# A two-block transformer on one core: from looped stages and three weight slots to an unrolled job list, five to eight slots and products that stream 512 weight columns

## The reference

```python
for l in range(2):                                    # first block
    x = layer_norm(ALPHA * x + 0.5 * swiglu(x, ffn1_w_gu[l], ffn1_w_down[l]))   # d_ff = 2816
    x = layer_norm(ALPHA * x + hybrid_mixer(x, w_in[l], w_out[l]))   # window attention + retention, w_in 1024x2816
    x = layer_norm(ALPHA * x + 0.5 * swiglu(x, ffn2_w_gu[l], ffn2_w_down[l]))
for l in range(2):                                    # second block, conditioned by c
    shift, scale, gate = split(silu(c) @ w_ada[l] + b_ada[l])
    h = x * (1 + scale) + shift
    p = h @ w_in_2[l]          # 4584 columns: latents, keys, queries, values, indexer, gate
    # latent attention (6 heads), dilated attention (6), top-64 sparse attention (4)
    y = concat(o_a, o_b, o_c) * silu(p_gate)
    x = layer_norm(ALPHA * x + (1 + gate) * (y @ w_out_2[l]))
```

## Time and profile before

| what | value |
|---|---|
| runs | 1542.51, 1539.28, 1542.38 us; median 1542.38 us |
| profiled execution | span 1539.8 us from the first to the last instruction; mean granted TensorE clock 0.988 |
| what lies around the span | 2.6 us, median of the runs less the span |
| PE busy | 1476.3 us, 96% of the span |
| PE weight loads | 1393.8 us, beside the products |
| DVE busy | 959.0 us, 62% |
| ACT busy | 621.4 us, 40% |
| POOL busy | 146.5 us, 10% |
| DMA | 265.49 MB, mean 172 GB/s |

### The profile page before, as it was taken

How to read it: one execution, slowest core, us unless ns; L and a number is a source line. 1 busy time by engine, 2 the same in 40 slices (tenths; PEclk the granted TensorE clock), 3 DMA queues, 4 the chain that set the end, 5 groups by cost and what they waited for, 6 DMA issues and landing times.

```text
span 1539.8 us, 29184 instructions
## 1 busy us (share of the span) xinstructions
PE 1476.3 (96%) x10900; PEld 1393.8 (91%) x10900; DVE 959.0 (62%) x1198; ACT 621.4 (40%) x754; POOL 146.5 (10%) x175
## 2 busy tenths in 40 slices
PE   8999999999999989999999999999999898999896
PEld 8999989889999989999898899999899896999794
DVE  2667665476677546676654766775657655567555
ACT  2434435523433414343355234333245463245551
POOL 1011010410011010100104100110100000000000
PEclk9999999999999999999999999999999999999998
DMA  7767645336767536676453366676453263453430
GB/s 247 230 215 232 216 150 168 111 110 212 228 209 231 184 131 227 218 232 215 148 171 110 110 212 226 212 230 200 158 172 113 78 206 97 136 184 96 126 120 28
DMA packets 195769, 265.49 MB, mean 172 GB/s; under 512 B 14992, under 2 KB 171152, under 8 KB 195168
## 3 DMA queue, kind: packets, MB, share of 16 engines
q1 hardware_dynamic: 183664, 222.51, 44.5%
q0 software_dynamic: 11728, 39.62, 8.4%
q10 hardware_dynamic: 288, 2.10, 0.4%
HBM read 263.13 MB, written 1.07 MB: 172 GB/s over the span
## 4 chain that ended last, share of the span: by engine, by line
PE 47%; issue 45%; POOL 5%; DVE 2%; DMA 1%; POOLq 0%; ACT 0%; DVEq 0%
PE ps L578 15%; PE ps L576 15%; PE ps L577 15%; PE ps L584 2%; POOL small L1653 1%; PE ps L716 1%; DVE x L1305 1%; POOL arena L1697 1%; PE ps L660 1%; POOL small L1726 1%; DMA mod_rows<-mod 0%; POOL arena L1698 0%; POOL arena L1699 0%; DVE arena L1555 0%; POOL arena L1695 0%
## 5 line engine op out<-in xcount | busy, mean ns | idle before, releaser
L1246 DVE TENSOR_TENSOR w_lo<-w_raw,w_hi 128x2048 fp32r<-128x2048 f32 (+3 forms) x224 | 489.2, 2188 | 261.5 <-ACT w_hi L995 257.2
L576 PE MATMUL ps<-col_hi,w_hi 128*128 128x256 f32 (+1 forms) x1744 | 493.6, 283 | 2.3 <-DVE w_lo L1246 2.3
L577 PE MATMUL ps<-col_lo,w_hi 128*128 128x256 f32 (+1 forms) x1744 | 492.3, 282 | 0.0
L578 PE MATMUL ps<-col_hi,w_lo 128*128 128x256 f32 (+1 forms) x1744 | 492.3, 282 | 0.0
L995 ACT ACTIVATE w_hi<-w_raw 128x2048 fp32r<-128x2048 f32 (+3 forms) x224 | 404.9, 1809 | 144.5 <-PE ps L578 140.6
L576 PEld LDWEIGHTS ps<-col_hi,w_hi 128*128 128x128 f32 x1744 | 334.9, 192 | 5.6 <-issue 3.3
L577 PEld LDWEIGHTS ps<-col_lo,w_hi 128*128 128x128 f32 x1744 | 335.0, 192 | 1.4
L578 PEld LDWEIGHTS ps<-col_hi,w_lo 128*128 128x128 f32 x1744 | 335.0, 192 | 0.0
L576 PE MATMUL ps<-w_hi,col_hi 128*128 128x256 f32 (+2 forms) x832 | 254.6, 306 | 4.1 <-DVE col_lo L1257 3.8
L577 PE MATMUL ps<-w_lo,col_hi 128*128 128x256 f32 (+2 forms) x832 | 250.2, 301 | 0.0
L578 PE MATMUL ps<-w_hi,col_lo 128*128 128x256 f32 (+2 forms) x832 | 250.1, 301 | 0.0
(11 more groups left out here) (150 smaller groups left out, 1240.3 us busy)
## 6 DMA issues: line engine op xcount, KB each, us to landing
w_raw<-in_ffn_w_gu SPq DMA_DIRECT2D x88, 1024.0 KB, 5.6
w_raw<-in_w_in SPq DMA_DIRECT2D x54, 1024.0 KB, 5.4
w_raw<-in_ffn_w_down SPq DMA_DIRECT2D x44, 1024.0 KB, 4.9
mod<-in_w_ada POOLq DMA_DIRECT2D x32, 768.0 KB, 5.3
w_raw<-in_w_out SPq DMA_DIRECT2D x16, 1024.0 KB, 4.9
norm_g<-in_ln_g POOLq DMA_DIRECT2D x8, 512.0 KB, 4.1
norm_b<-in_ln_b POOLq DMA_DIRECT2D x8, 512.0 KB, 5.6
w_raw<-in_w_uq SPq DMA_DIRECT2D x6, 576.0 KB, 4.0
```

The costliest lines, as they stand in the source:

```text
L576: pe.matmul(dst, a_hi, b_hi, start=start, stop=False)
L577: pe.matmul(dst, a_hi, b_lo, start=False, stop=False)
L578: return pe.matmul(dst, a_lo, b_hi, start=False, stop=stop)
L1246: tt(w_lo[slot][:, 0:n], raw[slot][:, 0:n], w_hi[slot][:, 0:n].bitcast(F32), ALU.subtract)\
```

## The change

The file is rewritten around one list of jobs, `JOBS`, made by `ffn_jobs`, `mix1_jobs` and `mix2_jobs`; every engine walks through the whole list without loops. Semaphore targets are counted beforehand.

- **Products.** Gate/up: 128 tokens are stationary and one unit holds 512 rows of d_model by 256 gate and 256 up columns, so a product streams 512 columns. The hidden rows then come out by token, and four transpositions a round (`ht`) are added. Mixer projections stream 512 columns where they can; others 424, 384, 288 or 256. The transposed projections of mixer two keep their form.
- **Ring.** `w_lo` has the same place as `w_raw`, so a slot is 16 KB a partition, and there are seven slots in feed-forward stages, six in mixer one, five in mixer two. The load of a unit waits for the last use of the unit that had the slot; the split of a unit is put into the job list of both ACT and DVE by `split_places`, 5120 streamed columns behind that last use. Both engines do it at that place, before the job that stands there.
- **Stages by tile.** The last four down units of a feed-forward stage are multiplied for tile 0, its norm starts, then for tile 1; the transposition of the next stage's tile 0 stands before the last unit of tile 1. In the mixers the output units are ordered alike, and the group norm goes by tile. The filling products are gone but for nine at the start. The next stage's first two units (or more) are multiplied for tile 0 before tile 1 is transposed.
- **Condition.** POOL folds scale and shift into the norm's factors (`fold`), the norm writes h, and x itself is made a little later (`xlate`).
- In mixer two the latent attention comes first, then the dilated, then the sparse one. The powers, the top-64 search and the attention steps are the same operations; each projection and x are copied and loaded by tile.
- The kernel is built with `dynamic_dma_scratch_size=8192`, which makes room for the slots.

```diff
-SLOTS = 3
+TAIL = 4
...
-MOD_CHUNKS = 2 * (ROUNDS - 3)
+MOD_CHUNKS = 16
+MOD_STEPS = MOD_CHUNKS // 2
...
-MIX1_WALK = (
-    [("unit", 0), ("unit", 1), ("unit", 2), ("rope1",), ("unit", 3), ("trqk",),
-     ("unit", 4), ("score", 0), ("unit", 5), ("unit", 6), ("turn", 0), ("score", 1), ("unit", 7), ("mix", 0),
...
-IDLE_IN, IDLE_OPEN = 3200, 7000
-IDLE_COND, IDLE_COND_SPLIT = 7500, 3500
-IDLE_START = 6000
-IDLE_RETMIX, IDLE_GATED = 1000, 2000
...
+BLOCKS = {"mix1": {"KV": ([("KV", 0)], 0, 256, (4, 4), (0, 256)),
+                   "QA": ([("QA", 0), ("QA", 1)], 0, 512, (5, 1), (0, 0)),
+                   "QR": ([("QR", 0), ("QR", 1)], 0, 512, (0, 5), (0, 0)),
+                   "KR": ([("KR", 0), ("KR", 1)], 0, 512, (4, 5), (0, 0)),
...
+        if name[0] == "gu":
+            _, r, h = name
+            w = f"ffn{f}_w_gu"
+            return 4, 512, [(w, l, h * 512, r * FU, FU, 0), (w, l, h * 512, F + r * FU, FU, FU)]
+        return 2, D, [(f"ffn{f}_w_down", l, name[1] * FU, 0, D, 0)]
...
+def ffn_jobs(s):
+    gu = lambda r, i: [("gu", s, r, i, h) for h in range(2)]
+    down = lambda r, i: [("down", s, r, i)]
+    jobs = gu(0, 0) + gu(1, 0) + [("xt", s, 1)] + gu(0, 1)
+    jobs += [("gu", s, 1, 1, 0), ("ht", s, 0), ("gu", s, 1, 1, 1), ("params", s)]
+    lag = 0
+    for r in range(2, ROUNDS):
+        jobs += gu(r, 0)
+        jobs += [("ht", s, r - 1)]
+        if 2 <= r < 2 + MOD_STEPS:
+            jobs += [("modsum", s, r - 2)]
+        jobs += gu(r, 1)
+        if 2 <= r < 2 + MOD_STEPS:
+            jobs += [("spread", s, r - 2)]
+        if lag < ROUNDS - TAIL:
+            jobs += down(lag, 0) + down(lag, 1)
+            lag += 1
+        if 2 <= r < 2 + MOD_STEPS:
+            jobs += [("modrow", s, r - 2)]
+    if s == FIRST2 - 1:
+        jobs += [("modload", FIRST2), ("gains", FIRST2), ("fold", FIRST2)]
+    tail = list(range(ROUNDS - TAIL, ROUNDS))
+    jobs += down(tail[0], 0) + down(tail[1], 0) + [("ht", s, ROUNDS - 1)] + down(tail[2], 0) + down(tail[3], 0)
+    jobs += [("norm", s, 0)]
+    for r in tail[:-1]:
+        jobs += down(r, 1)
+    return jobs + [("xt", s + 1, 0)] + down(tail[-1], 1) + [("norm", s, 1)]
+
+
...
+    jobs += [("ycols", s, 0, 0), ("retmix", s, 0), ("retmix", s, 1), ("out", s, 0, 0)]
+    jobs += [("retmix", s, 2), ("retmix", s, 3), ("ycols", s, 1, 0), ("gn", s, 0), ("out", s, 1, 0), ("gn", s, 1)]
+    jobs += [("out", s, 0, 1), ("ycols", s, 0, 1), ("ycols", s, 1, 1)]
+    jobs += [("out", s, 2, 0), ("out", s, 3, 0), ("norm", s, 0)]
+    return jobs + [("out", s, 1, 1), ("out", s, 2, 1), ("xt", s + 1, 0), ("out", s, 3, 1), ("norm", s, 1)]
...
+    jobs = r("L0", 0) + r("L1", 0) + [("xt", s, 1), ("xlate", s, 0), ("sq", s, 0)] + r("L0", 1) + [("xlate", s, 1)]
...
+    jobs += [("swish", s, 0), ("swish", s, 1)] + gate(0, 0) + y(0, 0) + mix("B", 2) + out(0, 0)
+    jobs += gate(0, 1) + gate(1, 0) + y(0, 1) + turn("C", 0) + score("C", 1) + y(1, 0) + out(1, 0) + gate(1, 1) + mix("C", 0)
+    jobs += gate(0, 2) + y(1, 1) + turn("C", 1) + out(0, 1) + mix("C", 1) + y(0, 2) + out(2, 0) + gate(1, 2)
+    jobs += out(3, 0) + [("norm", s, 0)] + out(1, 1) + y(1, 2) + out(2, 1)
...
+SLOTS_OF = {"ffn": (0, 1, 2, 3, 4, 5, 6), "mix1": (0, 1, 2, 3, 4, 7), "mix2": (0, 1, 2, 3, 4)}
+SPLIT_BEHIND = 5 * 1024
+IDLE_START = 2000
...
+def split_places():
+
+    places, at = [[] for _ in JOBS], 0
+    for n, u in enumerate(UNITS):
+        if AFTER[n] is None:
+            due = max(0, n - 1) * UNIT
+        else:
+            assert LAST_USE[UNITS[AFTER[n]]] < FIRST_USE[u]
+            due = STREAMED[LAST_USE[UNITS[AFTER[n]]] + 1] + SPLIT_BEHIND
+        while at < FIRST_USE[u] and STREAMED[at] < due:
+            at += 1
+        assert at <= FIRST_USE[u]
+        places[at].append(n)
+    return places
+
...
+            raw.append(sb(f"w_raw{j}", [P, UNIT], F32, first)[0])
+            w_lo.append(sb(f"w_lo{j}", [P, UNIT], F32R, first)[0])
...
+            def rows_by(n, j, group, i, dst, a_hi, a_lo, kts, cols, start, stop):
+                hi, lo = parts_of(n)
+                tok = slice(i * P, (i + 1) * P)
+                for k, kk in enumerate(kts):
+                    last = three(dst, a_hi[:, kk, tok], a_lo[:, kk, tok], hi[:, k, cols], lo[:, k, cols],
+                                 start and k == 0, stop and k == len(kts) - 1)
+                signal_end(last, n, j, group if stop else None)
+
...
-            def condition(st):
-
-                dve.wait_ge(mod_in, 16 * (st.layer + 1))
-                for i in range(TT):
-                    steps.wait(stt(y[:, i, :], mod[:, D:2 * D], 1.0, x[:, i, :], ALU.add, ALU.mult))
-                    tt(y[:, i, :], y[:, i, :], mod[:, 0:D], ALU.add).then_inc(sg["h_ready"], 1)
...
+                if s < LAST and KIND[s + 1] == "mix2":
+                    if i == 0:
+                        dve.wait_ge(folded, at["fold", ("fold", s + 1)])
+                    steps.wait(stt(h_rows[:, i, :], y[:, i, :], mu, scale2, ALU.subtract, ALU.mult))
+                    dve.wait_ge(rstd_ready, at["rstd", ("norm", s, i)])
+                    stt(h_rows[:, i, :], h_rows[:, i, :], rstd[:, i:i + 1], shift2, ALU.mult, ALU.add).then_inc(h_ready, 1)
...
+                    steps.wait(pool.tensor_scalar(scale2, scale2, 1.0, None, ALU.add))
+                    steps.wait(pool.tensor_tensor(spare, halves(scale2), halves(norm_b[:, :]), ALU.mult))
+                    pool.tensor_tensor(halves(shift2), halves(shift2), spare, ALU.add)
+                    pool.tensor_tensor(scale2, scale2, norm_g[:, :], ALU.mult).then_inc(folded, 1)
```

2406 lines of the change are left out of this document (1111 added, 1295 removed), and 11 rows, old and new, of the table BLOCKS.

## The result

The changed kernel takes 1590.43 us, the median of four runs (1588.97 to 1591.62), against 1542.45 us for the kernel before on the same chip: 1.0309 times as long, 95% interval 1.0285 to 1.0332. The prediction was 1495, with a range of 1445 to 1555 and 0.15 for slower. It missed the side and the size, by 95 us.

The account below looks back on a forecast made before the run. PE's instructions and the holes between them bound the kernel. Products -80.7, transpositions +19.2, filling -61.6, changes of form +6 and waits +70.5 gave -46.6 from 1542.38: 1495 us, own range 1470 to 1520, 8-in-10 range 1445 to 1555.

Parts of the forecast that it names:

- Filling: Products nobody reads, on PE: nine stay at the start, 2.0 us instead of 63.6, -61.6; unfilled time returns as waiting.
- Products: PE's matrix products: the same columns in fewer, wider products take 1156.7 us instead of 1237.4, 80.7 less.
- Waits: PE's waits after the change, listed place by place: 134 us together, against 63.5 us of idle time before.
- The group norm: Mixer one, after the last retention product: PE waits 12.4 us for tile 1's columns, before the change 1.7.
- the seven seams: Between stages: tile 1's columns late by 2.2 us each, 15 in all; two feed-forward stages after a mixer lose 10 more.
- The gated y of mixer two: Mixer two: gated y waits 7 us behind the swish and exponentials on ACT, part of 17.5 a mixer.
- rival B: Feed-forward rounds: the conditioning piece holds products in 32 rounds through the spreading product, 2.3 us each; 1568 us, chance 0.13.
- The start: Kernel start: 24 us of waits, bounds 15 to 30; first four units load-bound, PE starts near 16 us.
- 4 for order: Mixer two: 4 us listed for order, beside 17.5 us of waits in each of two mixers.
- Transpositions: Feed-forward rounds: 176 added, four in each of 44 rounds, at 0.11 us a start, +19.2 us.
- C: Rival, no change: waits inside the mixers twice those listed, 1543 us; shown by PE idle over 190 us; chance 0.10.
- the first term: The products' saving of 80.7 us; to be shown by 512-wide starts 0.227 apart and PE busy below 1400 us.

Follow-up runs that it names:

- the aligned kernel: The changed kernel with `small` 24 words shorter, so weight slots 0 to 4 begin at a multiple of 128 bytes: 1579.43 us, ratio 1.0216.

## Why the prediction was wrong, by its own steps

- **Filling (-61.6, "no gain by itself").** This step failed. It priced the fill as time in which PE had nothing to do, and put what the fill did besides at nothing. It also held the clock: 36.5 us in the changed kernel (fill put back), some 20 in the one before (fill taken out). The prediction's list of what could go another way did not have it, though its own row for the end shows the granted clock at 0.64 where PE idles.
- **Products (-80.7).** 23 of it did not come: 512-wide products start 0.2325 us apart at full clock. 18 of this (0.2325 - 0.2280) is the new allocation, which puts five slots at another address; 5 is the price itself, read from a stretch at 0.2268 in a kernel that averages 0.2275. The sign that the prediction named for this term, starts further apart than 0.227, came. The Trainium skill's rule that the prediction weighed, 2.5 ns a product ("TensorE: Matmul & The Clock Gate", section "Wait — 56ns, not 53.3ns?"), was wrong for the kernel before (13 ns by the starts) and nearer for this one (5 ns of the kernel's time for two in place of one).
- **Waits (134).** Measured 173.7; this term was too small by 40. The group norm (12.4, measured 11.4) and the end (11, measured 10.5) held, and the seven seams took 18 us in late columns where 15 and 10 were listed. The gated y of mixer two waited 31.6 / 2 = 15.8 us a mixer where the list had 7. Not on the list were the spreading product's 21.9, which rival B had in every round and the trace has in nine places; moving it gave back 20.6. The start was 24 and took 7.4 + 13.7 + 1.8 + 5.0 = 27.9 of idle time beside 4.2 of fill, and the first product came at 27.05, not 16: parameters that nobody needs yet share the load with unit 0. That seven weight units start at once was not what held it; holding five of them back left unit 0 where it was. The "4 for order" in mixer two is in no term of the 134.
- **Transpositions, the fold and `xlate`.** The middle of a feed-forward stage is 139.08 of 140.00 us busy, so the transpositions open no hole there. Four of them cost (106.63 - 105.95) - 0.2265 = 0.45 us, 0.11 each as priced, in the aligned kernel's trace, where they start at 105.95 and the second product behind them at 106.63. The fold is not quite free: its four operations take POOL 13 us, and beside them two weight splits on DVE take 3.13 and 3.85 us instead of 2.29. PE waits 3.0 us at 1137.0 for the `lat_lo` behind the first of these splits; most of that is the split's load, which came late, and 0.8 us is the slower split. No hole stands at `xlate`.
- The sum: 39.7 in holes, some 37 in clock and 23 in the price of a product make 100, of the 94.6 us between 1590.4 and 1495.8; some 6 us of other work came cheaper than priced.
- **The chances.** Slower had 0.15, all by waits. The case that came, three causes of 20 to 40 us each, was not among the rivals. PE's idle time stayed under the 190 us that would have shown C, and its busy time, at 1413.5, over the 1400 that would have shown the first term.

## What to carry to other kernels

Products that nobody reads are not free to delete: before a hole is left open, count what the clock costs behind it, and read the starts of products there, since such a stretch counts as busy. Put the fill in a bank that nobody waits for: in the other bank it added 5 to 7 us at each of five places. Read the price of an instruction again when the allocation changes, and look at which bytes a buffer starts at: a shift of the weight slots moved this kernel by 11 us, and the one before by 17, of which some 10 are the products' starts. At time zero, ask what is loaded beside the first weights: parameters for later cost this kernel's first unit 6 us.
